# Expert loop of a one-core decoder layer: tokens gathered for two pairs of experts at once and merged, both with fp32r products of a rounded part and a rest; routing weight applied to the expert activations; merge of a pair moved into the next pair

## The reference, cut to what matters

```python
h = layer_norm(DEEPNORM_ALPHA * h + mixed, ln1_g[l], ln1_b[l])
moe = hier_moe(h, router_g[l], ..., expert_w_gate[l], expert_w_up[l], expert_w_down[l])
h = layer_norm(DEEPNORM_ALPHA * h + moe, ln2_g[l], ln2_b[l])

def hier_moe(x, rg, rg_b, re, re_b, wg, wu, wd):
    ...
    for e in range(N_EXPERTS):                       # 16 experts
        h = jax.nn.silu(t @ wg[e]) * (t @ wu[e])     # 1024 -> 512, twice
        out = out + combine[:, e:e + 1] * (h @ wd[e])  # 512 -> 1024
```

## Time and profile before

| | us |
|---|---|
| three runs: median (lowest to highest) | 524.52 (523.69 to 528.94) |
| span of the profiled execution, first to last instruction | 522.5 |
| mean granted TensorE clock of the profiled execution | 0.978 |
| from the first gate matmul of the loop to the first instruction after it | 275.32 to 510.66 |

### The profile page before, as it was taken

The page is one execution under the profiler, slowest core; times in us unless marked ns, Lnnn a source line. Parts: engine busy times, 40 slices in busy tenths (PEclk is TensorE's granted clock), DMA queues, the critical chain, the costliest instruction groups (busy, mean ns, idle before and its releaser), DMA issues.

```text
span 522.5 us, 6332 instructions
## 1 busy us (share of the span) xinstructions
PE 478.6 (92%) x2478; PEld 300.7 (58%) x2478; DVE 287.3 (55%) x497; ACT 148.2 (28%) x223; POOL 165.2 (32%) x94
## 2 busy tenths in 40 slices
PE   7799999997979868769789999999999999999990
PEld 7689998875757756647673434344443434344440
DVE  6069968999999987983552321414031321414136
ACT  3075455554175285322311010101010010101010
POOL 8927707198583909743330000000000000000002
PEclk9999999998999998999999999999999999999996
DMA  7990455545551657459955999999999999999932
GB/s 267 261 355 3 160 182 182 181 161 189 182 174 44 219 211 290 162 170 369 382 205 188 389 386 387 386 387 384 386 387 387 387 387 387 386 387 387 386 133 81
DMA packets 76984, 142.92 MB, mean 274 GB/s; under 512 B 6776, under 2 KB 11009, under 8 KB 76960
## 3 DMA queue, kind: packets, MB, share of 16 engines
q1 hardware_dynamic: 75728, 140.29, 74.8%
q10 hardware_dynamic: 752, 2.11, 1.0%
q0 software_dynamic: 480, 0.20, 0.3%
HBM read 141.54 MB, written 1.05 MB: 273 GB/s over the span
## 4 chain that ended last, share of the span: by engine, by line
PE 61%; DVE 31%; DMA 3%; ACT 2%; issue 2%; SPq 0%; ACTq 0%; DVEq 0%
PE bank L1269 21%; PE bank L1294 11%; DVE ring L1505 7%; PE bank L1235 6%; PE bank L1308 5%; DVE rounded L1426 4%; DVE work L1606 4%; PE bank L1166 4%; PE bank L922 3%; PE bank L951 3%; DMA ring<-in_w_in_dram 3%; DVE ring L1603 2%; DVE ln1p L1463 2%; DVE rounded L1554 2%; PE bank L964 1%
## 5 line engine op out<-in xcount | busy, mean ns | idle before, releaser
L1269 PE MATMUL bank<-ring,gates 128*64 128x512 f32 x512 | 111.6, 594 | 0.4 <-ACT gates L864 0.4
L1040 PE MATMUL bank<-rounded 128*128 128x512 f32 x384 | 94.4, 401 | 6.5 <-POOL rounded L578 4.7
L1040 PEld LDWEIGHTS bank<-rounded 128*128 128x128 f32 x384 | 71.6, 191 | 25.5 <-POOL rounded L578 5.0
L613 POOL TENSOR_TENSOR work<-work,lnp 128x512 f32<-128x512 f32 x1 | 1.3, 1319 | 248.6 <-ACT work L877 248.6
L1269 PEld LDWEIGHTS bank<-ring,gates 128*64 128x64 f32 x512 | 36.2, 137 | 74.3 <-issue 74.3
L1759 DVE TENSOR_TENSOR gates<-gates,bank 128x512 f32<-128x512 f32 x8 | 5.5, 688 | 96.5 <-PE bank L1269 96.5
L1294 PE MATMUL bank<-ring,gates 128*64 128x512 f32 x256 | 58.5, 599 | 0.0
L578 POOL TENSOR_TENSOR rounded<-ring,rounded 128x1024 fp32r<-128x1024 f32 x16 | 39.9, 2524 | 25.1 <-ACT rounded L706 25.1
L586 POOL TENSOR_TENSOR gates<-gates,ring 128x1024 f32<-128x1024 f32 x8 | 34.9, 4360 | 36.0 <-ACT gates L749 36.0
L1235 PEld LDWEIGHTS bank<-gates,work 128*128 128x128 f32 x288 | 34.7, 192 | 13.7 <-issue 13.0
L1235 PE MATMUL bank<-gates,work 128*128 128x128 f32 x288 | 39.3, 281 | 0.7 <-DVE gates L1688 0.7
(11 more groups left out here) (245 smaller groups left out, 618.7 us busy)
## 6 DMA issues: line engine op xcount, KB each, us to landing
ring<-in_expert_w_down_dram SPq DMA_DIRECT2D x32, 1024.0 KB, 14.3
ring<-in_expert_w_up_dram SPq DMA_DIRECT2D x32, 1024.0 KB, 14.2
ring<-in_expert_w_gate_dram SPq DMA_DIRECT2D x32, 1024.0 KB, 14.3
ring<-in_w_in_dram SPq DMA_DIRECT2D x10, 2048.0 KB, 8.5
ring<-in_w_branch_dram SPq DMA_DIRECT2D x2, 2048.0 KB, 8.9
ring<-in_w_out_dram SPq DMA_DIRECT2D x2, 2048.0 KB, 10.7
ring<-in_w_in_dram SPq DMA_DIRECT2D x3, 1024.0 KB, 12.8
ring<-in_b_gate_dram SPq DMA_DIRECT2D x8, 256.0 KB, 4.4
```

The source lines that it names most:

```text
L1040: last = pe.matmul(bank[:, b, :], hT_part[hpart][:, k, b * P:(b + 1) * P], w[wpart][:, k, :], start=(k == 0 and hpart == wpart), stop=(k = ...
L1269: last = pe.matmul(bank[CAP * e:CAP * e + CAP, part // 2, :], xg[:, FC * h + k, CAP * e:CAP * e + CAP], w[:, e, k, :], start=(h == 0 and k ...
```

## The change

- **Gather.** `disp` now holds four experts (two pairs), so tokens are picked once for two pairs. `work` is split into `h1hi` (its value rounded to fp32r, copied by ACT) and `h1lo` (the rest, subtracted on GpSimd), and PE multiplies both with `disp` in fp32r: 32 matmuls of 256 columns for two pairs in place of 64 fp32 matmuls of 128 columns. PSUM holds a quarter of the result in each bank, so the picked tokens go out in four copies with waits between them. The first gather stands ahead of the loop, the later ones in every second pair.
- **Weights.** The dispatch is no longer multiplied by the routing weight. A small matmul brings the weight of each slot to a column (`wslot`), and DVE applies it in the instruction that multiplies silu and up.
- **Merge.** The expert output is split into `yhi` (ACT) and `ylo` (DVE). A pair's merge is 8 fp32r matmuls and stands in the next pair, behind its up part; the last merge stands behind the loop. The first merge multiplies zeros, which GpSimd writes earlier.
- **Moved.** `comb` is made at the head of each pair. The copy of the turned activations goes from DVE to ACT. The residual's scaling stands behind the last copy of the first gather on DVE, and PE waits for it at the head of the loop. Statistics of both halves are taken after the loop. The last normalisation's rows go into `ln1p`.

```diff
@@ GpSimd
+            pool.wait_ge(s_mix, 4 * NB)
+            pool.memset(comb[:, :, :].bitcast(F32), 0.0).then_inc(m_zero, 1)
+            pool.memset(moe_r[:, moe_at[0] - 2 * D:moe_at[0]].bitcast(F32), 0.0).then_inc(m_ylo, 1)
             pool.wait_ge(s_lnp, 64)
             for t in range(TB):
                 pool.wait_ge(s_zT, t + 1)
                 affine(t, work, ln1p, s_h1)
+            for t in range(TB):
+                pool.wait_ge(s_h1hi, t + 1)
+                pool.wait_ge(s_rtT, TB)
+                pool.tensor_tensor(h1lo[:, t, :], work[:, t, :], h1hi[:, t, :], ALU.subtract).then_inc(s_h1lo, 1)
@@ ScalarE
+            for t in range(TB):
+                act.wait_ge(s_h1, t + 1)
+                act.activation(h1hi[:, t, :], work[:, t, :], ACT.Copy).then_inc(s_h1hi, 1)
...
+            for b in (0, 2):
+                act.wait_ge(m_xg, b + 1)
+                gathered(b)
@@ TensorE
+            def gather(b):
+
+                for k in (2 * b, 2 * b + 1):
                     for t in range(TB):
...
+                        for part in (h1hi, h1lo):
+                            last = pe.matmul(bank[:, 2 + b % 2, (k % 2) * 2 * P:(k % 2 + 1) * 2 * P],
+                                             part[:, t, k * P:(k + 1) * P],
+                                             disp[:, t].rearrange("p e s -> p (e s)"),
...
+            def merge(before, half):
+
+                for t in range(TB):
+                    for part in (yhi, ylo):
+                        last = pe.matmul(bank[:, MERGED_IN[2 * half + t], :], comb[:, before % 2, t * P:(t + 1) * P],
...
             pe.wait_ge(m_disp, 1)
-            pe.wait_ge(s_h1, TB)
-            gather(range(KC))
+            pe.wait_ge(s_h1hi, TB)
+            pe.wait_ge(s_h1lo, TB)
+            gather(0)
+            gather(1)
+            pe.wait_ge(m_xga, 1)
+            gather(2)
+            pe.wait_ge(m_xgd, 1)
+            gather(3)
...
-                    pe.wait_ge(m_xga, it + 1)
+                    own = disp[:, :, 2 * (j % 2):2 * (j % 2) + 2, :].bitcast(F32)
+                    pe.wait_ge(m_acc, it * 4 + 2)
+                    pe.wait_ge(m_wcur, it + 1)
...
+                    pe.wait_ge(m_silu, it + 1)
+                    pe.wait_ge(m_cTo, it + 1)
+                    for half in range(2):
+                        pe.wait_ge(m_ylo, it * 2 + half)
+                        merge(j + 1, half)
...
+                        if j % 2:
+                            pe.wait_ge((m_xga, m_xgd)[half], group * 2 + 3)
+                            gather(2 + half)
...
+            pe.wait_ge(m_acc, pairs * 4 + 2)
+            for half in range(2):
+                pe.wait_ge(m_ylo, pairs * 2 + half)
+                merge(BODY + 1, half)
@@ VectorE
+            pair_weights(0)
+            for b in (1, 3):
+                dve.wait_ge(m_xg, b + 1)
+                gathered(b)
             dve.wait_ge(s_h1, TB)
             for t in range(TB):
-                dve.tensor_scalar(acc[:, t, :], work[:, t, :], ALPHA, None, ALU.mult)\
-                    .then_inc((m_stat, m_acc)[t], 1)
...
-            dve.wait_ge(m_xg, 1)
-            gathered()
+                dve.tensor_scalar(acc[:, t, :], work[:, t, :], ALPHA, None, ALU.mult).then_inc(m_acc, 1)
...
+            pairs = dve.snap(npass * PAIRS)
+            dve.wait_ge(m_acc, pairs * 4 + 2)
             dve.wait_ge(s_lnp, 96)
+            for i in range(4):
+                half, t = divmod(i, 2)
+                dve.wait_ge(m_c, pairs * 4 + i + 1)
+                link(merged(i))
+                half_stats(t, acc[:, t, half * HALF:(half + 1) * HALF], half)
+                if half:
+                    row_var(t, 2)
```

More of the change, by code:

```diff
@@ L1259, in weights @@
                         return expert_slot(s)
-                    pe.wait_ge(m_xga, it + 1)
+                    own = disp[:, :, 2 * (j % 2):2 * (j % 2) + 2, :].bitcast(F32)
+                    pe.wait_ge(m_acc, it * 4 + 2)
+                    pe.wait_ge(m_wcur, it + 1)
+                    for t in range(TB):
+                        pe.transpose(bank[:, 7, t * P:(t + 1) * P], own[:, t].rearrange("p e s -> p (e s)"),
+                                     ident[:, :])
+                    for t in range(TB):
+                        last = pe.matmul(bank[:, 7, TB * P:TB * P + 2], own[:, t].rearrange("p e s -> p (e s)"),
+                                         wcur[:, t, :], start=(t == 0), stop=(t == TB - 1))
+                    last.then_inc(m_cT, 1)
                     for part in range(4):
-                        if part == 1:
-                            pe.wait_ge(m_xgd, it + 1)
+                        if part < 2:
+                            pe.wait_ge(m_xga, group * 2 + 1 + part)
+                            pe.wait_ge(m_xgd, group * 2 + 1 + part)
                         h = part % 2
```

231 lines of the change are left out of this document (122 added, 109 removed).

## The result

The changed kernel takes **534.98 us** in the median of 4 runs (533.9 to 538.61), the kernel before 526.18 us (4 runs, 523.69 to 528.94). The ratio is **1.0193, 95% interval 1.0157 to 1.0229**: 1.9% slower, and beyond the 1% that a measurement of this kernel can tell. (The quotient of the two medians is 1.0167; that is outside too. The forecast was 534.0.

A forecast was written before the change was run, and what follows sets the result against it. PE and the DMA engines were both taken as full, the memory 3.3 us ahead at the end. Span 522.5 + 8.6 + 1.2 − 3.3 + 3.2 = 532.2, plus 2.0 to the median: 534 us, range 528.5 to 538.5.

The forecast's parts named there:

- Part 1, the loop: In the loop: PE needs about 26 us a pair, but only 3.3 us can be taken; the rest becomes waiting for weights.
- Part 2, ahead of the loop: Before the loop: first gate matmul at 283.9 instead of 275.32, +8.6 us, 3.9 on DVE and 4.7 order and added steps.
- The stall: Routing on DVE: instructions with two SBUF operands wait for GpSimd's two subtractions, +3.9 us, bounds 0 and 4.8.
- Part 3, the clock: At the loop's start: PE runs at half clock after little work, first slot back later, +1.2 us, bounds 0 to 3.5.
- Part 4, the end: Behind the last down part: 9.0 us to the last statistics instead of 5.8, +3.2 us, bounds 2.5 and 4.
- the cushion: End of the loop: PE begins the last down part 3.3 us after its transfer lands, the most the kernel can gain there.
- The sum: Whole kernel: 522.5 + 8.6 + 1.2 − 3.3 + 3.2 = 532.2 us span, median 2.0 above, 534 us.
- No stall on DVE: Routing: 40-column instructions slip through beside GpSimd, start moves by 4.7 us only and the clock holds, 529.1 us; chance 0.17.
- The matmuls count in full: Loop: weights arrive in time regardless, so it shrinks by 26 us, total 511 us; chance 0.03.
- The clock falls in the loop: Last part and merges: PE's clock falls after waits, 3.6 us and more, with 3.5 at the start, 541 us; chance 0.10.

The follow-up runs named there:

- half the bytes: Half the weight bytes for the 40 parts loaded inside the loop, same matmuls: changed kernel 517.36 us, ratio 0.9837; kernel before 525.58 us, ratio 0.9985.
- early start: Changed kernel with the first gather writing four PSUM banks instead of two and residual scaling off PE's path: 531.63 us, ratio 1.0108.
- first half's statistics: Changed kernel, last four pairs written out, no gather for a nonexistent group, last pair's first half merged and its statistics taken during the second: 531.83 us, ratio 1.0104.
- no dummy gather: Changed kernel with the last four pairs written out behind the loop and the gather for a nonexistent group left out: 533.1 us, ratio 1.0143.
- warm: Changed kernel with more idle transposes on PE ahead of the loop, 58 instead of 24 and 20 after the first gather: 534.37 us, ratio 1.0159.
- combined kernels: Changed kernel with subtractions on VectorE and start and end edits together: 525.45 us, ratio 0.9972; again with both subtractions behind the dispatch: 524.97 us, ratio 0.9986.

## Why the prediction held, step by step

**Part 1, the loop.** It held. The saved matmuls bought waiting: 15.0 us at the gate and up parts, in nine waits, most of 1.77 us (about 1.9 was forecast), the first at the 32nd part, 421.4 us (after 29 was forecast), the rate 387 GB/s for 386. The two kernels with half the bytes show the cause: PE's own need per pair is 26.5 us, and only the weight stream hides it. The forecast had put PE's saving too high, at 26 us for the loop where 19.3 showed, which did no harm, since either is far more than the 3.3 us that can be taken. The early start shows the other half, that the start of the stream moves the end one to one: 210.0 us from the first issue to the last up part, with an issue 4.5 us sooner behind the dispatch.

**Part 2, ahead of the loop.** 8.6 us were forecast for the first gate matmul and 8.2 came. The stall was forecast at 3.9 us: the two instructions cost 3.3 in the profiled execution and 3.9 in five other traces; without the subtractions the kernel is 5.8 us (3 to 8.5) faster, so the term is shown, and its size within 3 to 8.5. (The forecast took the subtractions to begin at 266.00 and the routing 0.6 us behind them; in the five traces the routing comes earlier and meets both from their start.) Of the rest of the term the early start took 2.8 back (two waits and the scaling), and 1.7 more at the slow first part. The Trainium skill, GPSIMD Engine Reference, section 1 (Specifications), names the shared SBUF interface with VectorE as the cause of such contention. The traces agree: instructions with two SBUF inputs took 1.46 and 2.27 us for 0.20, a reduction of one input between them its 0.20. They add that the price goes by GpSimd's instruction and not by VectorE's 40 columns.

**Part 3, the clock.** 1.2 us were forecast. It was 1.7 in the profiled execution (first gate part 5.4 us instead of 3.7), 1.9 without the subtractions, 1.7 with the first half's statistics, and 0 in three other traces that keep this order at the start or shorten it (early start, no dummy gather, half the bytes). It is a term that falls in some executions and not in others, and no single figure is right for it.

**Part 4, the end.** The tail was forecast at 9.0 us and took 8.5, +2.7 for +3.2. The step that failed stands in the forecast's sum as the cushion: it let PE start on the last down part as it lands (509.9 forecast, 509.6 measured). But PE still had 12.7 us of work between the last up part's landing (498.9) and that start, the gather for a group that doesn't exist among it, and began at 511.7. So of the 3.3 us of cushion 2.1 were lost again. The kernel without the dummy gather shows that this is the cause: there PE waits 0.3 us for the last down part and begins on it 10.9 us behind the start of the last up part instead of 12.7, 1.8 sooner. With the 0.6 us that its tail is shorter (7.9 for 8.5) that makes the 2.5.

**The sum.** On the span: 8.2 + 1.7 for the start, −3.3 + 2.1 for the cushion, +2.7 for the tail, 11.4 in all, for 11.1 measured (533.6 less 522.5). The forecast had 9.7: 2.6 more were lost at the last down part and the clock, 0.9 less at start and tail. From the span to the median it was 1.4 instead of 2.0. And the median before rose by 1.7 us with a fourth run, so that the two medians lie 8.8 us apart where 9.5 was forecast. So the agreement to 1 us is in part luck: errors that offset each other.

**The rivals.** "No stall on DVE" falls by the traces and by the kernel without the subtractions. "The matmuls count in full" falls by the pair with half the bytes, which shows what it would have needed. "The clock falls in the loop" falls: with 198.63 of 218 us busy and waits of 1.77 us before parts of 3.65, the clock stayed at 1.00 to the end. The Trainium skill, TensorE: Matmul & The Clock Gate, section "HAM oscillation", tells of a loop fed by DMA that falls to half clock at each wait; its waits are longer than these, and no run here shows them.

## What to carry to other kernels

Where two resources are full at once, ask which has the lead and how much of it is left at the end: that lead (here 3.3 us of 231) is all that a relief of the other can bring. In a loop fed by a ring, time ahead of the first freed slot and behind the last landing is on the path one to one, so work moved there from the loop is work moved onto the path, even if the loop's engine gets 19 us lighter. Serial work that the loop does for a next round that never comes is free while there is slack, and lies on the path as soon as the last transfer is the bound.

## What the runs showed of the hardware

A VectorE instruction of 128x40 with two SBUF operands beside a GpSimd instruction of 128x1024 was held until that one had ended (its own end lies 0.1 us behind or less), each time: 1.15 and 1.16, 1.29, 1.46, 2.03 to 2.06, and 2.27 to 2.29 us for 0.20; two in a row met two GpSimd instructions in a row. Reductions of one operand between them kept their 0.20, and so did the bias addition, which has one operand in PSUM. The stall works in both directions: GpSimd's instruction took 3.23 us for 2.35 beside a long VectorE subtraction, which itself took 1.94 for 1.22.

The memory stream was the same, to 0.2 us, in the traces of the changed kernel and of its variants that load all the bytes and keep the order within a pair: from the first ring issue to the start of the last up part 210.0 us (changed kernel, early start), 210.1 (warm), 209.8 (without the dummy gather), 210.2 (without the subtractions; first half's statistics). In the combined kernels, where a pair's turns stand behind its first gate part, it is 210.9 and 210.6.
